# A decoder step with expert retrieval: expert slots in groups of two instead of four, causal key blocks, picks in parts, stages placed by weight

## The chip, the cores and the metric

One core of a Trainium2 chip runs the whole program. The metric is the device time of one execution in microseconds. The page and the traces come from one execution that the hardware profiler recorded.

## The reference

One layer of a decoder for a prompt of 1024 tokens and for 8 sequences of one new token each. All data are float32. For the prompt (the sample goes the same way, with 2048 cached keys for each sequence):

```
xn = rmsnorm(xp)                               # 1024 wide
h  = xn @ w_in                                 # 2240 columns: query latent, key/value latent, rotary key, three conv parts
q_lat, q_rope, ckv, kr = ...                   # 4 heads, latent of 256, rotary part of 64
s = q_lat . ckv + q_rope . kr, masked: key <= query;  p = softmax(s);  o = p @ ckv
xp = xp + concat(norm(o @ w_uv), norm(short_conv(...))) @ w_o
x  = rmsnorm(xp)
q  = x @ w_query                               # 8 heads x 2 halves x 128
s  = q . sub_keys                              # 8 x 2 x 128 scores
sv, si = top_k(s, 16)                          # of each half
top_s, pos = top_k(sv0[:, None] + sv1[None], 16)
experts = si0 * 128 + si1 at pos;  g = softmax(top_s)
u = expert_u[experts];  v = expert_v[experts]  # 8 x 16 = 128 rows of 1024 for each token, twice
a = gelu(x . u)
xp = xp + sum over 128 of (g * a) * v
```

The 128 chosen rows of `expert_u` and the 128 of `expert_v` are 4 KB each, and every token has its own. Outputs are both token groups after a last norm, the new key latents, the new rotary keys and the conv states.

## The kernel before

The prompt is cut into 8 tiles of 128 tokens; a ninth tile holds the 8 sample tokens. Each tile has a **front** (norm, projections, conv, attention, output mix, second norm, eight queries with their top 16, the look-up of the expert numbers) and a **peer** part (128 slots; a slot is one chosen expert of each of the 128 tokens). The front of tile `it+1` is woven into the peer part of tile `it`; the front of tile 0 stands alone at the start, and the sample's small peer part stands alone at the end.

A slot needs two gathers of 512 KB, issued by Pool as indirect DMAs (L1448): rows of `expert_u` into `u_ring`, rows of `expert_v` into `v_ring`, each a ring of `RING` = 8 slots. VectorE multiplies a `u` slot with the tokens and sums (`dot_group`, L1310, which frees the slot in `u_ring`), ScalarE applies gelu, VectorE multiplies with the gates (`weigh_group`, L1316), ScalarE makes a diagonal matrix of it (L933), and TensorE multiplies it with the `v` slot into the accumulator `acc` (`v_group`, L684, which frees the slot in `v_ring`). All of this goes in groups of `G` = 4 slots, 32 groups a tile, with dots one group ahead.

Pool (L1451 to L1471) issues four `u` gathers of the next group, then four `v` gathers of this group, each after a wait for its ring place (`u_free`, `v_free`). It waits for `picked_moved` before slot 0 and for `picks_moved` before slot 64 of a tile.

The order on each engine is written out by hand and is the same on all of them: in group `g`, dots of `g+1` and weights of `g` on VectorE, then the stages of the front that belong to this group; on TensorE the stages, then `v_group(g)`; on ScalarE gelu of `g+1`, diagonals of `g`, then its share of the stages. `beside` (L85) spreads the 31 stages of a prompt front over the first 30 of the 32 groups, one to a group whatever they cost, and the 62 of the sample's front over 31 groups. So `mix_out` is one stage with four weight pieces (L560), a query one stage, a head of the attention one stage, and the last selection (L1245) comes in group 29. The engines wait for each other inside a stage, and each works in order, so whatever follows in its queue waits too.

The attention of the prompt takes all 1024 keys in every tile, with a mask (L1102); keys not yet written are zero from three memsets (L1443). SP loads the weights as 21 pieces a tile, 20 of 1024 KB and one of 768 KB, through a ring of three (`load_w`, L317).

Between tiles VectorE copies the gates and the new tokens to their place (`move_on`, L1318), does two groups of dots, the last norm (`finalize`, L1342) and moves the second half of the picks (`move_picks`, L1331). Seven prompt tiles run in a loop of the engine's own (`Fori`), the eighth is written out.

Before the first gather the opening does all of front 0: projections, four heads, the mix, eight queries and both selections.

## Time and profile before

| | |
|---|---|
| median of three runs | 3765.8 us (3758.39 to 3769.8) |
| the profiled execution | 3753.85 us |
| its span, first to last instruction | 3751.9 us |
| TensorE matmul busy | 2708.7 us (72%), 13848 instructions |
| TensorE weight loads busy | 1557.8 us (42%) |
| VectorE busy | 2310.8 us (62%), 5393 instructions |
| ScalarE busy | 838.7 us (22%) |
| Pool busy | 2332.5 us (62%), 2071 instructions |
| moved | 1321.00 MB, a mean of 352 GB/s over the span |
| mean granted TensorE clock | 0.848 |

Busy time is the time of an engine's instructions; the rest of the span it waits for others or between instructions. DMA share is the part of the time in which the 16 DMA engines had packets under way; it can read slightly over 1 where packets overlap. A row of the timeline gives start, length, engine, line and operation, and in brackets how long the engine had been idle before it and for whom it waited.

### The profile page before, as it was taken

Reading aid. Unit: us, or ns where it says so; the run is one execution under the profiler, and the core shown is the slowest. Engines: PE = TensorE matmul, PEld = TensorE weight load, DVE = VectorE, ACT = ScalarE, POOL = GpSimd, SP = SyncE. Lnnn points to the kernel's source line nnn. Section 1 sums busy time; section 2 is a strip of 40 time slices with the busy share of each in tenths; the row PEclk is TensorE's granted clock in tenths of the full one; section 3 lists DMA queues with packets and bytes.
Section 4 is the critical chain, followed back from the end, with each engine's and each line's share of the span. In section 5 each row is a group of like instructions: output and inputs, shape, how many; then the busy total and the mean of one; then the engine's idle time right before and its main releaser. Section 6 shows DMA issues by size and latency. Waiting matters only on the chain.

```text
span 3751.9 us, 47864 instructions
## 1 busy us (share of the span) xinstructions
PE 2708.7 (72%) x13848; PEld 1557.8 (42%) x13848; DVE 2310.8 (62%) x5393; ACT 838.7 (22%) x2103; POOL 2332.5 (62%) x2071
## 2 busy tenths in 40 slices
PE   7738875687658865797568765887578776988874
PEld 5525442344324532444235432544244433644351
DVE  2374668555875578566865677566856686344474
ACT  1111311222122311232132212131123212123211
POOL 0027776766767676767767776676676776555542
PEclk9878987898878987899779987898889987799876
DMA  5149999999999999999999999999999999999884
GB/s 182 67 161 412 368 401 391 367 400 358 411 359 411 355 404 362 396 372 401 409 348 410 363 411 349 408 361 382 384 376 393 379 409 370 330 331 313 311 308 163
DMA packets 371757, 1321.00 MB, mean 352 GB/s; under 512 B 59684, under 2 KB 78670, under 8 KB 348424
## 3 DMA queue, kind: packets, MB, share of 16 engines
q0 software_dynamic: 297216, 1082.26, 75.2%
q1 hardware_dynamic: 70724, 229.76, 15.9%
q10 hardware_dynamic: 3524, 5.57, 0.4%
q8 instruction: 124, 2.03, 0.2%
q14 instruction: 169, 1.38, 0.1%
HBM read 1311.82 MB, written 5.62 MB: 351 GB/s over the span
## 4 chain that ended last, share of the span: by engine, by line
PE 32%; DVE 32%; DMA 14%; issue 12%; ACT 6%; POOL 2%; SPq 1%; DVEq 1%; ACTq 0%; POOLq 0%
DVE u_ring L1310 12%; PE acc L684 11%; DMA v_ring<-in_expert_v,pick_cur 7%; PE front L410 5%; DMA u_ring<-in_expert_u,pick_cur 4%; PE front L517 3%; PE front L566 3%; PE front L538 2%; ACT diag L933 2%; DVE sv L1201 2%; PE front L518 2%; DVE si_u L1202 2%; DVE work L1201 1%; DMA w_ring<-in_w_pieces 1%; DVE work L1202 1%
## 5 line engine op out<-in xcount | busy, mean ns | idle before, releaser
L1448 POOL DMA_INDIRECT v_ring<-in_expert_v,pick_cur x1024 | 1206.2, 1178 | 687.3 <-PE acc L684 422.4
L684 PE MATMUL acc<-v_ring,diag 128*64 128x512 f32 x4096 | 1188.3, 728 | 592.4 <-ACT diag L933 419.3
L1448 POOL DMA_INDIRECT u_ring<-in_expert_u,pick_cur x1024 | 1106.7, 1081 | 666.2 <-issue 290.5
L1310 DVE CUSTOM_DVE_ANT_0 u_ring<-u_ring,xn_cur 128x1024 f32<-128x1024 f32 x1024 | 1210.6, 1223 | 268.8 <-DMA u_ring<-in_expert_u,pick_cur 253.7
L684 PEld LDWEIGHTS acc<-v_ring,diag 128*64 128x64 f32 x4096 | 348.9, 164 | 1269.2 <-issue 686.6
L410 PE MATMUL front<-work,w_ring 128*128 128x128 f32 (+1 forms) x4896 | 607.2, 283 | 7.0 <-DVE work L1194 5.6
L410 PEld LDWEIGHTS front<-work,w_ring 128*128 128x128 f32 x4896 | 593.0, 201 | 41.6 <-issue 32.6
L926 ACT ACTIVATE gelu<-dots 128x4 f32<-128x4 f32 x256 | 52.7, 206 | 1834.2 <-DVE dots L1310 1833.4
L933 ACT ACTIVATE diag<-ident,wgt 128x64 f32<-128x64 f32 x1024 | 271.5, 336 | 120.7 <-DVE wgt L1316 120.7
L566 PE MATMUL front<-w_ring,work 128*128 128x256 f32 (+1 forms) x576 | 149.7, 426 | 75.5 <-DVE work L1169 65.9
L566 PEld LDWEIGHTS front<-w_ring,work 128*128 128x128 f32 (+1 forms) x576 | 116.2, 205 | 113.3 <-issue 64.2
L1201 DVE MAX8 sv<-work 128x8 f32<-128x128 f32 (+1 forms) x288 | 83.0, 288 | 120.5 <-ACT work L915 103.5
L538 PE MATMUL front<-work,ckv_rows 128*128 128x128 f32 x1024 | 132.6, 292 | 23.2 <-ACT work L879 23.2
L538 PEld LDWEIGHTS front<-work,ckv_rows 128*128 128x128 f32 x1024 | 126.8, 205 | 43.0 <-issue 42.0
L517 PE MATMUL front<-ckvT,rows_next 128*128 128x512 f32 x256 | 125.0, 611 | 1.2 <-ACT rows_next L874 1.2
L417 PE MATMUL front<-ident,work 128*128 128x128 f32 (+1 forms) x72 | 16.8, 408 | 143.7 <-DVE work L1023 143.7
L1102 DVE SCALAR_TENSOR_TENSOR work<-low_keys,small,front 128x512 f32<-128x512 f32 x64 | 45.0, 744 | 101.8 <-PE front L518 101.8
L926 ACT ACT_TABLE_LOAD x83 | 106.5, 1283 | 1.5
L1130 DVE COPY rows_next<-front 128x512 f32<-128x512 f32 x32 | 22.1, 691 | 131.2 <-PE front L624 131.2
L1178 DVE TENSOR_TENSOR rows_next<-front,x_t 128x512 f32<-128x512 f32 (+1 forms) x18 | 11.6, 685 | 125.7 <-PE front L566 125.7
L1202 DVE FIND_INDEX8 si_u<-sv,work 128x8 uint32<-128x128 f32 (+1 forms) x288 | 81.7, 284 | 2.4 <-issue 2.4
L1310 DVE DVE_READ_ACCUMULATOR2_ANT dots<- 128x1 f32 x1024 | 82.3, 80 | 0.0
(242 smaller groups left out, 2382.9 us busy)
## 6 DMA issues: line engine op xcount, KB each, us to landing
w_ring<-in_w_pieces SPq DMA_DIRECT2D x180, 1024.0 KB, 8.4
u_ring<-in_expert_u,pick_cur POOLq DMA_INDIRECT x1024, 12.3
v_ring<-in_expert_v,pick_cur POOLq DMA_INDIRECT x1024, 10.7
work<-in_cache_ckv SPq DMA_DIRECT2D x64, 128.0 KB, 6.2
w_ring<-in_w_pieces SPq DMA_DIRECT2D x9, 768.0 KB, 7.5
x_t<-in_x_prompt SPq DMA_DIRECT2D x8, 512.0 KB
out_y_prompt<-work ACTq DMA_DIRECT2D x8, 512.0 KB
ckv_rows<-in_cache_ckv SPq DMA_DIRECT2D x32, 128.0 KB
```

The lines of the kernel that those rows point to most:

```text
L410: last = nc.tensor.matmul(dst, w[:, k, c0:c0 + m], xT[:, k * T:(k + 1) * T], start=(k == 0), stop=(k == DC - 1))
L517: nc.tensor.matmul(F[half][:, :], q_lat[:, c, h, :], ckvT[:, c, ks], start=(c == 0), stop=False)
L518: last = nc.tensor.matmul(F[half][:, :], q_ro[:, h, :], krT[:, ks], start=False, stop=True)
L538: last = nc.tensor.matmul(F[4][:, c * P:(c + 1) * P], ckv_rows[:, j, c * P:(c + 1) * P], W[1][:, j * P:(j + 1) * P], start=(j == 0), stop= ...
L566: last = nc.tensor.matmul(dst, W[2][:, k * T:(k + 1) * T], w[:, k, :], start=(k == 0), stop=(k == DC - 1))
L684: last = nc.tensor.matmul(acc[rows, half, :], diag[:, s % RING, :], v_ring[:, s % RING, half * 512:half * 512 + 512], start=False, stop=(s ...
L926: nc.scalar.activation(gelu[:, g * G:(g + 1) * G], dots[:, g * G:(g + 1) * G], ACT.Gelu).then_inc(on.gelu_done, 1)
L933: nc.scalar.activation(diag[:, s % RING, :], ident2[:], ACT.Copy, scale=wgt[:, s:s + 1]).then_inc(on.diag_made, 1)
L1201: own(v.max(best, scores), held=True)
L1202: last = v.max_index(index[:, 8 * r:8 * r + 8], best, scores)
L1310: v.tensor_tensor_reduce(u_ring[:, slot, :], u_ring[:, slot, :], xn2_cur[:, block_of(r), :], 1.0, 0.0, ALU.mult, ALU.add, dots[:, g * G + ...
L1448: pool.indirect_dma_start(ring[:, slot, :], None, a[table][0], bass.IndirectOffsetOnAxis(ap=pick, axis=0)).then_inc(loaded[slot], 16)
```

## The change

It touches the order of the work and the attention's extent.

- **Groups of two.** `G` is 2, so 64 groups a tile. Dots run two groups ahead (`AHEAD` = 2, again four slots). Pool still issues bursts of four (`BURST`), `u` of the next four, then `v` of these. `RING` stays 8.
- **Causal key blocks.** Front `f` computes scores, maximum, exp, scaling, turns and values for its `f+1` key blocks of 128 alone; the three memsets go.
- **Finer stages.** The latent projection is three stages of one weight piece, each conv projection two, `mix_out` four. The conv input comes before the turn of the new keys.
- **Picks in parts.** Selection is done in parts of heads: 0 to 3 and 4 to 7 for tiles 1 to 8, and 0 to 1, 2 to 3, 4 to 7 for tile 0. A part's look-up, gates and picks are finished and copied at once, except the last part of tiles after the first, which is copied between the tiles as before. The opening only does the first part of tile 0; its other six queries and two selections are woven into tile 0's slots ahead of front 1.
- **Placing by weight.** `place` spreads the stages by costs in a table (`COST`), over the first 60 of the 64 groups of a prompt tile and the first 62 of the last.
- **Written out.** The loops of tiles are unrolled on all engines, with constants in the waits.
- The order of slots follows: a part's 32 or 64 slots come from its heads alone (`spread_blocks` pairs neighbouring picks).

```diff
-G = 4
+G = 2
 GROUPS = SLOTS // G
-RING = 2 * G
+RING = 8
+AHEAD = 2
+BURST = 4
+def parts_of(f):
+    return [(0, 2), (2, 4), (4, 8)] if f == 0 else [(0, 4), (4, 8)]
+def parts_done(f, part):
+    return sum(len(parts_of(e)) for e in range(f)) + part
+_FIRST = (["norm", "turn"] + [("latent", k) for k in range(3)] + ["latent_norm"] + [("z_in", k) for k in range(2)] + ["kv_rows"]
+          + [("z_gate", k) for k in range(2)] + [("conv", k) for k in range(2)] + ["q_proj", "q_latent"])
+_MIX = ["attn", "mix_norm"] + [("mix_out", k) for k in range(N_OUT)] + ["ffn_norm", "ffn_turn", ("query", 0)]
+COST = {"norm": 0.5, "turn": 0.3, "latent": 0.5, "latent_norm": 0.8, "z_in": 0.7, "kv_rows": 0.2, "z_gate": 0.7, "conv": 0.8, "q_proj": 0.6,
+        "q_latent": 0.4, "head": 1.1, "attn": 0.3, "mix_norm": 1.1, "mix_out": 0.5, "ffn_norm": 0.7, "ffn_turn": 0.3, "query": 0.95, "select": 1.5,
+        "pages": 0.8}
+def _part(f, part):
+    h0, h1 = parts_of(f)[part]
+    return [("query", h + 1) for h in range(h0, h1)] + [("select", part)]
+def front_of(f):
+    return _named(_FIRST + [("head", h) for h in range(H + 1)] + _MIX + _part(f, 0))
+def rest_of(f):
+    return sum([_part(f, part) for part in range(1, len(parts_of(f)))], [])
+def place(stages, span):
+    total, done, groups = sum(COST[s[2]] for s in stages), 0.0, [[] for g in range(GROUPS)]
+    for s in stages:
+        groups[min(int(done * span / total), span - 1)].append(s)
+        done += COST[s[2]]
+    return groups
+def plan(it):
+    if it < TILES - 1:
+        stages = [(0, P) + s for s in rest_of(0)] if it == 0 else []
+        return place(stages + [(it + 1, P) + s for s in front_of(it + 1) + rest_of(it + 1)], GROUPS - 4)
+    f = it + 1
+    stages = _named(_FIRST + [("pages", n) for n in range(SB * QUARTERS + QUARTERS)] + _MIX) + _part(f, 0) + rest_of(f)
+    return place([(f, SB) + s for s in stages], GROUPS - 2)
+def key_blocks(f, half):
+    return min(4, max(0, f + 1 - 4 * half))
...
                 for half in range(2):
-                    ks = slice(half * 512, half * 512 + 512)
+                    ks = slice(half * 512, half * 512 + key_blocks(f, half) * P)
+                    if ks.stop == ks.start:
+                        continue
+                    dst = F[half][:, 0:ks.stop - ks.start]
...
+                if h:
+                    pe.wait_ge(on.olat_kept, n)
                 for c in range(2):
-                    for j in range(TILES):
+                    for j in range(f + 1):
...
-                for g in range(GROUPS):
-                    stages = beside(g, T)
-                    before = 1 if has_pages(stages) else len(stages)
-                    for name, n in stages[:before]:
-                        stage(it + 1, T, name, n)
+                for g, stages in enumerate(PLAN[it]):
+                    for s in stages:
+                        stage(*s)
                     if T != P and g == GROUPS - 1:
                         turn_picks()
                     v_group(it, g)
-                    for name, n in stages[before:]:
-                        stage(it + 1, T, name, n)
...
-            with pe.Fori(0, TILES - 1) as it:
+            for it in range(TILES - 1):
...
-            def select(own, f, T):
+            def move_gates(f, part):
+                h0, h1 = parts_of(f)[part]
+                after(dve, on.w_made, (f - 1) * GROUPS + h1 * TOPK // G if f else 0)
+                return spread_blocks(gate_cur, gate_next, h0 * TOPK // 2, h1 * TOPK // 2)
+            def move_picks(f, part):
+                h0, h1 = parts_of(f)[part]
+                after(dve, on.v_free, RING + (f - 1) * SLOTS + h1 * TOPK if f else 0)
+                spread_blocks(pick_cur, pick_next, h0 * TOPK // 2, h1 * TOPK // 2).then_inc(on.picks_moved, 1)
+            def select(own, f, T, part):
+                hs = slice(*parts_of(f)[part])
...
-                look_up(own, T, 1)
+                look_up(own, T, hs)
...
+                if T == P and (f == 0 or part < len(parts_of(f)) - 1):
+                    assert f == 0 or weighed[0] >= (f - 1) * GROUPS + hs.stop * TOPK // G
+                    own(move_gates(f, part))
+                    move_picks(f, part)
...
             def tile(it, T):
-                own = Own(dve, on.dve_front, (it + 1) * DVE_FRONT)
-                for g in range(GROUPS):
-                    stages = beside(g, T)
-                    half = G // 2 if has_pages(stages) else G
-                    if g and g + 1 < GROUPS:
-                        dot_group(it, g + 1, 0, half)
+                for g, stages in enumerate(PLAN[it]):
+                    if g and g + AHEAD < GROUPS:
+                        dot_group(it, g + AHEAD)
                     if g:
                         weigh_group(it, g)
...
                 if T == P:
-                    move_on(own2, it + 1)
+                    move_on(own, it + 1)
                     dot_group(it + 1, 0)
                     total_square(it, P)
-                    dot_group(it + 1, 1)
+                    for g in range(1, AHEAD + 1):
+                        dot_group(it + 1, g)
                     weigh_group(it + 1, 0)
...
-            pool.memset(ckv_rows[:], 0.0).then_inc(on.zeroed, 1)
-            pool.memset(ckvT[:], 0.0).then_inc(on.zeroed, 1)
-            pool.memset(krT[:], 0.0).then_inc(on.zeroed, 1)
...
-                pool.wait_ge(on.picked_moved, it + 1)
-                gather_group(it, 0, "expert_u", u_ring, u_loaded)
-                for g in range(GROUPS):
-                    if g + 1 < GROUPS:
-                        gather_group(it, g + 1, "expert_u", u_ring, u_loaded)
-                    gather_group(it, g, "expert_v", v_ring, v_loaded)
+                gather_burst(it, 0, "expert_u", u_ring, u_loaded)
+                for first in range(0, SLOTS, BURST):
+                    if first + BURST < SLOTS:
+                        gather_burst(it, first + BURST, "expert_u", u_ring, u_loaded)
+                    gather_burst(it, first, "expert_v", v_ring, v_loaded)
```

## Rows read from the trace of the kernel before

**Rows 1.** The page, moved bytes per second in 40 equal slices of the span.
```profile
GB/s 182 67 161 412 368 401 391 367 400 358 411 359 411 355 404 362 396 372 401 409 348 410 363 411 349 408 361 382 384 376 393 379 409 370 330 331 313 311 308 163
```

**Rows 2.** The page, DMA queues: packets, MB, share of 16 engines.
```profile
q0 software_dynamic: 297216, 1082.26, 75.2%
```

**Rows 3.** Chain of work: start us, us, what; the first projection of each front.
```profile
286.13 10.91 PE front L410 x95
...
3159.86 14.75 PE front L410 x96
```

**Rows 4.** Stretches of the span: length, busy (instructions) by engine, clock, DMA share, GB/s.
```profile
286.13:3159.86 2873.73, 2072.86 (x10368) 1157.36 (x10368) 1895.48 (x4324) 665.67 (x1714) 2017.84 (x1793) 0.86 0.99 385
3159.86:3240.00 80.14, 79.07 (x428) 65.32 (x429) 20.56 (x56) 11.64 (x36) 35.11 (x33) 0.64 0.88 330
3240.00:3514.00 274.00, 239.74 (x1389) 121.90 (x1389) 126.18 (x271) 75.73 (x173) 156.79 (x133) 0.92 0.94 323
3514.00:3690.00 176.00, 127.82 (x610) 74.21 (x609) 119.43 (x350) 31.54 (x87) 80.23 (x69) 0.74 0.72 267
```

**Rows 5.** The same view, 12 us stretches of one tile.
```profile
690.00:702.00 12.00, 10.45 (x54) 6.40 (x55) 7.17 (x15) 2.64 (x7) 6.55 (x8) 0.72 0.95 362
...
834.00:846.00 12.00, 12.00 (x58) 6.05 (x55) 8.21 (x14) 3.95 (x8) 8.49 (x7) 1.00 0.89 314
846.00:858.00 12.00, 8.80 (x49) 5.94 (x48) 10.62 (x21) 4.46 (x10) 8.24 (x6) 0.82 0.83 281
...
942.00:954.00 12.00, 9.92 (x51) 5.13 (x46) 9.76 (x30) 1.15 (x6) 9.58 (x8) 0.72 1.02 413
...
1062.00:1074.00 12.00, 4.22 (x12) 0.94 (x8) 11.52 (x20) 1.27 (x1) 5.89 (x5) 0.64 0.65 221
1074.00:1086.00 12.00, 8.59 (x32) 2.82 (x32) 9.32 (x20) 3.54 (x11) 9.56 (x9) 0.79 0.85 279
```

**Rows 6.** Timeline of Pool, the first gather.
```profile
256.54 1.50 POOL L1448 DMA_INDIRECT u_ring<-in_expert_u,pick_cur  x1 [251.37 <-DVE pick_cur L1226]
```

**Rows 7.** Timeline of VectorE, two heads of the opening.
```profile
106.53 1.40 DVE L1102 SCALAR_TENSOR_TENSOR work<-low_keys,small,front 128x512 f32<-128x512 f32 x2 [5.48 <-PE front L518]
...
109.23 0.15 DVE L1107 TENSOR_SCALAR small<-small 128x1 f32<-128x1 f32 x1
...
118.57 1.41 DVE L1102 SCALAR_TENSOR_TENSOR work<-low_keys,small,front 128x512 f32<-128x512 f32 x2 [5.48 <-PE front L518]
```

**Rows 8.** Timeline of TensorE, opening: the turn of the new keys.
```profile
38.34 0.69 PE L453 MATMUL front<-ident,ck_t 128*128 128x128 f32 x2 [5.28 <-DVE ck_t L1054]
```

**Rows 9.** Timeline of VectorE, opening: queries two and three begin.
```profile
187.50 0.30 DVE L1201 MAX8 sv<-work 128x8 f32<-128x128 f32 x1
...
194.40 0.30 DVE L1201 MAX8 sv<-work 128x8 f32<-128x128 f32 x1
```

**Rows 10.** Timeline of VectorE, opening: one step of a look-up.
```profile
246.03 1.23 DVE L1240 TENSOR_TENSOR work<-work,iota 128x1024 f32<-128x1024 f32 x1
```

**Rows 11.** The page, groups of instructions: busy us, mean ns, idle before.
```profile
L684 PE MATMUL acc<-v_ring,diag 128*64 128x512 f32 x4096 | 1188.3, 728 | 592.4 <-ACT diag L933 419.3
...
L566 PE MATMUL front<-w_ring,work 128*128 128x256 f32 (+1 forms) x576 | 149.7, 426 | 75.5 <-DVE work L1169 65.9
```

**Rows 12.** Groups of instructions, Pool engine, one tile (698.67 to 1108.99).
```profile
L1448 POOL DMA_INDIRECT v_ring<-in_expert_v,pick_cur x129 | 149.4, 1158 | 83.5 <-PE acc L684 49.9 <-issue 33.6
L1448 POOL DMA_INDIRECT u_ring<-in_expert_u,pick_cur x128 | 139.0, 1086 | 44.1 <-issue 36.6 <-DVE dots L1310 6.3 <-PE acc L684 1.2
```

**Rows 13.** Timeline of Pool beside a group of dots: start us, us.
```profile
960.23 0.94 POOL L1448 DMA_INDIRECT u_ring<-in_expert_u,pick_cur  x1 [0.30 <-issue]
961.47 1.77 POOL L1448 DMA_INDIRECT u_ring<-in_expert_u,pick_cur  x1 [0.30 <-issue]
963.55 1.98 POOL L1448 DMA_INDIRECT u_ring<-in_expert_u,pick_cur  x1 [0.30 <-issue]
```

**Rows 14.** Timeline of VectorE, the first of those four dots.
```profile
961.20 1.22 DVE L1310 CUSTOM_DVE_ANT_0 u_ring<-u_ring,xn_cur 128x1024 f32<-128x1024 f32 x1
```

More of the change, by code:

```diff
@@ L72 @@
 QP = NPAGES // QUARTERS
-_FIRST = ["norm", "turn", "latent", "latent_norm", "kv_rows", "z_in", "z_gate", "conv", "q_proj", "q_latent"]
-_LAST = (["attn", "mix_norm", "mix_out", "ffn_norm", "ffn_turn"] + [("query", h) for h in range(PH // 2 + 1)] + [("select", 0)]
-         + [("query", h) for h in range(PH // 2 + 1, PH + 1)] + [("select", 1)])
-STAGES_PROMPT = _FIRST + [("head", h) for h in range(H + 1)] + _LAST
-STAGES_SAMPLE = _FIRST + [("pages", n) for n in range(SB * QUARTERS + QUARTERS)] + _LAST
@@ L80, in stages_of @@
-def stages_of(T):
-    return [s if isinstance(s, tuple) else (s, 0) for s in (STAGES_PROMPT if T == P else STAGES_SAMPLE)]
-def beside(g, T):
-    stages = stages_of(T)
-    span = GROUPS - 2 if T == P else GROUPS - 1
-    return [s for i, s in enumerate(stages) if i * span // len(stages) == g]
+def parts_of(f):
[4 more added lines that the diff above has]
+          + [("z_gate", k) for k in range(2)] + [("conv", k) for k in range(2)] + ["q_proj", "q_latent"])
@@ new lines, with _named @@
+_MIX = ["attn", "mix_norm"] + [("mix_out", k) for k in range(N_OUT)] + ["ffn_norm", "ffn_turn", ("query", 0)]
+COST = {"norm": 0.5, "turn": 0.3, "latent": 0.5, "latent_norm": 0.8, "z_in": 0.7, "kv_rows": 0.2, "z_gate": 0.7, "conv": 0.8, "q_proj": 0.6,
+        "q_latent": 0.4, "head": 1.1, "attn": 0.3, "mix_norm": 1.1, "mix_out": 0.5, "ffn_norm": 0.7, "ffn_turn": 0.3, "query": 0.95, "select": 1.5,
+        "pages": 0.8}
+def _named(stages):
+    return [s if isinstance(s, tuple) else (s, 0) for s in stages]
@@ L95 @@
+def plan(it):
[5 more added lines that the diff above has]
+    return place([(f, SB) + s for s in stages], GROUPS - 2)
+PLAN = [plan(it) for it in range(TILES)]
 LAST = TILES - 1
-def has_pages(stages):
-    return any(name == "pages" for name, n in stages)
@@ L323, in load_tile @@
             def load_tile(f, T):
-                row = sp.snap(f * P)
+                row = f * P
                 load_x(f, T, row)
@@ L349, in _ @@
                 load_w(0, k)
-            with sp.Fori(1, TILES) as f:
+            for f in range(1, TILES):
                 load_tile(f, P)
@@ L788, in _ @@
             nc.tensor.transpose(acc[:, 0, 0:VEC_ROWS], stage_vec, ident[0:VEC_ROWS, 0:VEC_ROWS]).then_inc(on.vec_turned, 1)
-            for name, n in stages_of(P):
+            for name, n in front_of(0):
                 stage(0, P, name, n)
-                if name == "latent":
+                if name == "latent" and n == 2:
                     turn_weights()
@@ L1221, in spread_blocks, with look_up @@
             def spread_blocks(dst, src, first, end):
-                pairs = dst[:, :].rearrange("p (q j) -> p q j", j=2)
+                to = dst[:, :].rearrange("p (q j) -> p q j", j=2)
+                by = src[:, :].rearrange("p (q i) -> p q i", i=2)
                 for i in range(2):
                     for j in range(2):
-                        last = v.tensor_copy(pairs[i * HB:(i + 1) * HB, first:end, j],
-                                             src[j * HB:(j + 1) * HB, i * HB + first:i * HB + end])
-                return last
-            def look_up(own, T, half):
-                hs = slice(half * PH // 2, (half + 1) * PH // 2)
-                grid = [T, PH // 2, TOPK, TOPK]
+                        last = v.tensor_copy(to[i * HB:(i + 1) * HB, first:end, j], by[j * HB:(j + 1) * HB, first:end, i])
+                return last
+            def look_up(own, T, hs):
+                grid = [T, hs.stop - hs.start, TOPK, TOPK]
+                hit = W[0][:, 0:(hs.stop - hs.start) * TOPK * TOPK].rearrange("p (h k a) -> p h k a", k=TOPK, a=TOPK)
                 own(v.tensor_copy(si[0:T, hs], si_u[0:T, hs]))
@@ L1269, in stage @@
                     keep_turned(f, T)
-                elif name == "latent":
+                elif name == "latent" and n == 2:
                     square_latents(f, T)
@@ L1273, in stage @@
                     latents(own, f, T)
-                elif name == "z_gate":
+                elif name == "z_gate" and n == 1:
                     conv_in(own, f, T)
-                elif name == "conv":
+                elif name == "conv" and n == 1:
                     conv(own, f, T)
```

282 lines of the change are left out of this document (128 added, 154 removed).

## The prediction

> **What bounds it now.** I read the page's moved bytes first, then the queues, then stretches, and only then single engines. The reader is to see that from the fourth slice on the core moves 350 to 412 GB/s without a pause [rows 1], and that the gathers are 1082 of the 1321 MB [rows 2]. The chain of work gives the period: the same projection starts at 286.13 and seven tiles later at 3159.86, so a tile takes 410.5 us [rows 3]. Over those seven tiles the DMA share is 0.99 at 385 GB/s, while TensorE is busy 72% and VectorE 66% [rows 4]. A busy DMA can still be badly fed: in a good stretch of 12 us it moves 413 GB/s, in the bad ones 221 to 362 [rows 5]. Most of the 35 such stretches of that tile read 402 to 415, and I take 411 as the full rate. A tile moves 256 gathers of 512 KB, 21.8 MB of weights and 1.2 MB of inputs and outputs, 157.2 MB, which is 382.5 us at 411. So a tile loses 28 us to starved DMA engines. They sit in three places: the heads and the output mix (834 to 882: 2.8 and 3.8 us in the two shown, 12 in all four), the end of the tile with the last query, the selection and the move to the next tile (1062 to 1098 and 690 to 714: 5.5, 3.9 and 1.4 in those shown, 14.6 in all), and 2.4 between [rows 5]; each is 12 x (1 - rate/411).
>
> Around the tiles lie an opening without gathers until 256.54 [rows 6], and after 3159.86 another 592 us, of which 530 at 330, 323 and 267 GB/s [rows 4].
>
> **Opening.** Three edits move the first gather, and all three lie on the path, as Pool has nothing else to wait for [rows 6].
> - Heads. One head takes 12.04 us (106.53 to 118.57), most of it 1024 wide work and 5.48 us of waiting for scores [rows 7]. Front 0 now has one key block instead of eight. The hand-offs stay: five VectorE steps, an exp, a turn and the scores; the smallest step costs 0.15 us [rows 7]. The trace has no head this small, so from below eight such steps with a few hand-offs, 2 us, and from above a third of today's, 5 us. I take 3.3, nearer to the small step because all but the hand-offs shrink by eight: 4 x 8.7 = 35 us less (28 to 40).
> - The conv input comes before the turn of the keys, for which TensorE now idles 5.28 us [rows 8]: 5 less (0 to 6, if its weights are late).
> - Queries and selection. A query takes 6.9 us of VectorE (187.50 to 194.40) [rows 9]. The third begins at 194.40; in its place comes the selection of two heads: six look-up steps of half of 1.23 us [rows 10], 3.7, and some twenty small steps and copies of 0.15 to 0.3, about 4. So the gather comes at about 203 instead of 256.54: 53 less (50 to 56).
>
> Sum: 93 us less (78 to 102); the first gather at about 164. The three memsets on Pool lie under this opening and are worth nothing.
>
> **Tile 0 gets the rest.** Six queries (41 us) and two selections (8 and, with four heads, 12) now lie beside its slots: 61 us of VectorE in the first 13 or so of 64 groups, and six weight pieces, 6.3 MB or 15 us of DMA. Twenty-eight slots and this work ask for about 28 x 1.3 + 61 + weights, 100 us of VectorE; DMA needs 28 x 2.55 + 15 = 86. Cost 20 us: 15 from the bytes, the rest VectorE beyond the rings' slack (15 to 45).
>
> **Seven prompt tiles.** No bytes go, so 382.5 us is the floor. What can be had is the 28.
> - Heads: TensorE has no idle time there (12.00 of 12.00) [rows 5]; a head takes 12.04 us without slots [rows 7] and four slots of matmuls bring it to about 14, against 10.2 of gathers. With `f+1` blocks its 11 or so of TensorE shrink to (f+1)/8. At 2.2 groups a head that is 6 to 13 us for f = 1 to 5 and 14 to 15 for f = 6, 7, against 11.2 of gathers. The first five fronts are covered; the last two keep about 6 us of their loss.
> - Mix: four weight pieces in one group of four slots become four stages over four groups. TensorE's 16.6 us for them (149.7 over nine tiles) and 9.3 for the slots (1188.3 over 1024) [rows 11] then stand beside eight slots, 20 us of gathers and 10 of weights. Covered.
> - End of tile: the last selection goes from group 29 of 32 to 57 of 64, with twelve slots free of stages behind it instead of eight, and half of the picks are long there. But the selection is still one piece of 12 us in which VectorE does no dots, and the move between tiles still stands. I leave half of the 14.6.
> - Hand-offs: twice as many weights, gelus and waits, 32 x 0.2 us more on VectorE and ScalarE, hidden by their 30% and more of idle time [rows 4]; with that cover gone, 6 us a tile.
> - Pool is the cover that is thin. In the tile it is busy 288.4 us for 257 gathers, has 70.2 of issue between them and waits 57 [rows 12]; a gather takes 0.94 us alone and 1.77 and 1.98 beside dots [rows 13, 14]. So Pool alone needs 359 of 382.5 us. Splitting dots into pairs moves where they meet the gathers: from nothing to 0.5 us more for each of 64 pairs (0 to 32 us, so 359 to 391). I take the middle, 375: still under the floor, but Pool can't catch up after a stall.
>
> Together I leave 10 us a tile, and 16 for f = 6 and 7: 5 x 392.5 + 2 x 398.5 = 2759.5 against 2873.7 [rows 4], 114 less; with tile 0's 20, 94 less (10 to 170).
>
> The Trainium skill, page "SBUF — State Buffer", section "Who interferes with whom", has an operation of VectorE with two inputs in SBUF contend only with Pool instructions that read SBUF. The dots are such an operation, and the gathers beside them double, so the row is what I go by; by the rule the gathers would stay at 0.94 where they write only, and Pool would need 318.
>
> **The last tile and the end.** Its first 80 us are TensorE's (79.07 of 80.14, clock 0.64), the next 274 nearly so (239.74) [rows 4]. Splitting shares the projections' time out among slots but doesn't shorten it: 5 less each. In the 176 us that follow DMA share is 0.72; queries two to a group become one to about 2.2 slots: 15 less. The last 62 us stay. Sum 25 less (0 to 50).
>
> **Sum.** 93 + 94 + 25 = 212 less than the profiled execution's 3753.85 (span 3751.9, 2 us around it): 3542. The median of the three runs lies 12 above that execution, so 3554; I say 3550.
>
> **Rivals.**
> - Near the floor: rings and finer stages hide nearly all. Tiles at 384 (186 less), 15 for tile 0, 50 at the end: 3754 - 98 - 186 + 15 - 50 + 12 = 3447. For it: the good stretches; against: selection and the move between tiles remain whole. 0.13.
> - The chains only move: stages wait across engines as before, and lost time comes back where heads and queries now follow closely. Tiles at 405 (38 less), 40 for tile 0, opening 85, end 5: 3754 - 85 - 38 + 40 - 5 + 12 = 3678. For it: four waits of VectorE inside each head remain [rows 7], and Pool can't catch up. The change then does not do in the tiles what it says. 0.2.
> - Memory is the limit: reads of one core cannot go beyond what a tile's mean already shows, 385, so tiles keep 410.5 and only the opening counts: 3754 - 93 + 15 + 12 = 3688. Against: 413 over 12 us and 412 over a whole slice of 94 [rows 1, 5]. 0.02. The Trainium skill gives this rule in "SBUF — State Buffer", section "A bandwidth-pool intuition that's wrong (but worth ruling out)": about 358 GB/s from HBM for a core, and so 3690 us for 1321 MB; the trace disagrees, with 385 over 2874 us.
> - Slower, by Pool: if a pair of dots stretches as many gathers as a burst of four did, two by about 0.95 us each [rows 13], 64 pairs cost 122 us and Pool needs 318 + 122 = 440 a tile. Seven tiles then take 206 more: 3754 - 93 + 206 - 25 + 12 = 3854. It decides from about 427 us of Pool a tile, where the opening and the end are used up. Against: a stretched gather ends with the dots, and two dots last 2.4 us. 0.05.
>
> **Chances.** Forecast 0.6 (3480 to 3620), the others as given. Range 3440 to 3690: it takes in the first three rivals and leaves out the slow one and the tails. Within 0.3%, about what a measurement of this kernel can tell from no change, is 0.02; slower 0.05; faster 0.93.
>
> **What would show it.** First gather at 150 to 180. The same projection's period 388 to 400 for fronts 2 to 5 and more for 6 and 7; tile 0 some 20 longer. Stretches of 12 us under 350 GB/s gone from the heads, still there at the tile's end. Gathers' mean at 1.1 to 1.25 us; above 1.4, Pool has become the bound. TensorE's busy time less by the key blocks. It would be wrong if the period stays over 403, or if Pool has no waits left and the stretches read under 400.

## The result: 3869.7 us, 2.8% slower

The changed kernel takes 3869.7 us (median of four, 3861.4 to 3875.3), the kernel before 3763.0 beside it: ratio 1.028, 95% interval 1.026 to 1.031. The forecast was 3550 with a range of 3440 to 3690: the time lies outside the range, and the sign is wrong too.

The page of the changed kernel (busy time of the engines, and what the DMA moved in the 40 slices), the answer to [rows 1]:

```profile
PE 2687.4 (69%) x13192; PEld 1483.0 (38%) x13192; DVE 2297.9 (59%) x5733; ACT 899.1 (23%) x2374; POOL 2221.2 (57%) x2068
GB/s 177 206 353 377 359 340 307 411 367 381 332 411 359 394 362 355 379 333 382 339 410 314 380 366 348 365 309 385 333 407 294 372 370 338 284 320 294 308 328 202
```

Some work did go: TensorE has 21 us less. Pool has 111 us less with as many gathers; these took less time each, and the memsets are gone. But the slices of tiles 1 to 6 now swing between 294 and 411. In the chain of work stand the first projection of front 2 and, six tiles later, that of the sample's front (compare [rows 3]):

```profile
654.88 4.04 PE front L447 x32
...
3257.73 7.00 PE front L447 x32
```

That is six tiles of 433.8 us, where a tile had 410.5; "over 403" was the prediction's own sign of being wrong. The first gather came as forecast (timeline of Pool, answer to [rows 6]):

```profile
159.48 1.43 POOL L1469 DMA_INDIRECT u_ring<-in_expert_u,pick_cur  x1 [159.02 <-DVE pick_cur L1260]
```

Stretches of 12 us of one tile (busy time of each engine, clock, DMA share, GB/s), the answer to [rows 5]; good stretches still read 408 to 417:

```profile
2053.00:2065.00 12.00, 11.75 (x54) 5.94 (x50) 4.45 (x8) 4.25 (x7) 3.98 (x5) 0.92 0.76 285
2065.00:2077.00 12.00, 9.48 (x32) 4.62 (x33) 5.30 (x12) 3.02 (x8) 8.40 (x8) 0.86 0.66 223
2125.00:2137.00 12.00, 3.52 (x10) 1.28 (x12) 11.86 (x18) 1.49 (x7) 4.94 (x5) 0.57 0.61 225
2245.00:2257.00 12.00, 2.40 (x8) 0.59 (x6) 11.54 (x25) 0.94 (x4) 5.75 (x6) 0.64 0.75 288
2329.00:2341.00 12.00, 7.77 (x26) 2.72 (x28) 11.70 (x31) 3.66 (x16) 2.74 (x3) 0.62 0.34 119
```

These are two heads, the mix norm, the first selection and the last one. In the heads VectorE works 4.5 and 5.3 of 12 us, Pool 4.0 and 8.4, and in the second stretch TensorE isn't full either (9.5): the engines wait for each other. In the last stretch Pool works 2.7 us, on three gathers.

To compare kernels I cut each profiled run at the first gather and at the end of each tile's sum (ScalarE's copy of `acc`), all on chips where the kernel before takes about 3760 us:

| us | before | changed | changed, groups of four | changed, two edits |
|---|---|---|---|---|
| up to the first gather | 256.5 | 159.5 | 158.3 | 160.2 |
| tile 0 | 415.0 | 474.9 | 444.5 | 442.4 |
| tiles 1 to 6 | 2468.0 | 2606.8 | 2438.9 | 2398.0 |
| last tile and end | 612.4 | 627.4 | 637.8 | 606.0 |
| span | 3751.9 | 3868.5 | 3679.5 | 3606.5 |

And inside a tile, what each place lost by moving less than 411 GB/s, as the mean of tiles 1 to 6: the length of each place times (1 - rate/411), cut at the first scores, the attention's last step, the first and last output piece, and the last selection:

| us lost a tile | before | changed | groups of four | two edits |
|---|---|---|---|---|
| projections | 4.6 | 1.7 | 1.9 | 1.5 |
| heads | 7.9 | 18.2 | 7.0 | 4.0 |
| attention's last step, mix norm | 3.6 | 5.9 | 1.1 | 1.0 |
| output mix | 0.5 | 1.6 | 0.7 | 3.7 |
| queries, first selection | 2.1 | 11.0 | 0.5 | 0.5 |
| last selection to the end | 8.2 | 11.9 | 11.3 | 4.4 |
| sum | 26.9 | 50.4 | 22.4 | 15.2 |

The last two columns are experiments 13 and 17 below. Against groups of four the changed kernel loses 28 us more a tile: 11 in the heads, 10.5 between the last output piece and the last selection, 5 at attention's last step and the mix norm. The 11.0 us of the fifth row don't lie between the queries: the queries up to the first selection lose 0.3 together, though most of them too have a group without a stage between them. The first selection and the 12 us behind it lose 6.1, and the rest up to the last selection 4.5.

### The profile page after: what moved, and what is told of

Same layout as the page of the kernel before. It is cut to its first block, busy times and chain, and to the rows that moved or that the text cites. A ratio compares the mean times of both kernels' runs of the same rounds, so it can differ in the third digit from the quotient of the medians.

```text
span 3868.5 us, 43060 instructions
## 1 busy us (share of the span) xinstructions
PE 2687.4 (69%) x13192; PEld 1483.0 (38%) x13192; DVE 2297.9 (59%) x5733; ACT 899.1 (23%) x2374; POOL 2221.2 (57%) x2068
## 4 chain that ended last, share of the span: by engine, by line
PE 38%; DVE 32%; DMA 12%; issue 8%; ACT 6%; POOL 2%; SPq 2%; DVEq 0%; POOLq 0%; ACTq 0%
PE acc L726 17%; DVE u_ring L1354 10%; DMA v_ring<-in_expert_v,pick_cur 9%; PE front L447 6%; DVE si_u L1235 3%; PE front L608 2%; DVE sv L1234 2%; PE front L557 2%; DVE work L1235 2%; ACT diag L972 2%; DVE work L1234 2%; POOL u_ring L1469 1%; PE front L634 1%; DVE work L1273 1%; POOL v_ring L1469 1%
## 5 line engine op out<-in xcount | busy, mean ns | idle before, releaser
L726 PE MATMUL acc<-v_ring,diag 128*64 128x512 f32 x4096 | 1299.3, 770 | 954.4 <-ACT diag L972 753.3
L1469 POOL DMA_INDIRECT v_ring<-in_expert_v,pick_cur x1024 | 1128.8, 1102 | 769.2 <-PE acc L726 502.5
L1469 POOL DMA_INDIRECT u_ring<-in_expert_u,pick_cur x1024 | 1074.1, 1049 | 830.0 <-DVE dots L1354 381.6
L965 ACT ACTIVATE gelu<-dots 128x2 f32<-128x2 f32 x512 | 103.5, 203 | 1656.3 <-DVE dots L1354 1655.3
L1134 DVE SCALAR_TENSOR_TENSOR work<-low_keys,small,front 128x512 f32<-128x512 f32 (+3 forms) x48 | 28.0, 612 | 103.6 <-PE front L558 103.6
L957 ACT COPY work<-front 128x256 f32<-128x256 f32 (+1 forms) x72 | 25.1, 349 | 245.8 <-PE front L447 245.8
L634 PEld LDWEIGHTS front<-sub_keysT,work 128*128 128x128 f32 (+1 forms) x288 | 45.0, 221 | 97.0 <-issue 94.8
L1362 DVE TENSOR_TENSOR wgt<-gelu,gate_cur 128x2 f32<-128x2 f32 x512 | 78.8, 155 | 0.7
L557 PE MATMUL front<-ckvT,rows_next 128*128 128x512 f32 (+3 forms) x192 | 77.6, 530 | 2.3 <-ACT rows_next L910 2.3
L580 PE MATMUL front<-work,ckv_rows 128*128 128x128 f32 x576 | 74.8, 285 | 5.2 <-DVE work L1148 5.2
```

Source lines behind the costliest of these rows:

```text
L557: nc.tensor.matmul(dst, q_lat[:, c, h, :], ckvT[:, c, ks], start=(c == 0), stop=False)
L634: last = nc.tensor.matmul(F[1][0:T, c * KEYS:(c + 1) * KEYS], W[3][:, c * T:(c + 1) * T], sub_keysT[:, c, :], start=True, stop=True)
L726: last = nc.tensor.matmul(acc[rows, half, :], diag[:, s % RING, :], v_ring[:, s % RING, half * 512:half * 512 + 512], start=False, stop=(s ...
L965: nc.scalar.activation(gelu[:, g * G:(g + 1) * G], dots[:, g * G:(g + 1) * G], ACT.Gelu).then_inc(on.gelu_done, 1)
L1362: v.tensor_tensor(wgt[:, s], gelu[:, s], gate_cur[:, s], ALU.mult).then_inc(on.w_made, 1)
L1469: pool.indirect_dma_start(ring[:, slot, :], None, a[table][0], bass.IndirectOffsetOnAxis(ap=pick, axis=0)).then_inc(loaded[slot], 16)
```

## What happens between two heads

TensorE's timeline over one period of the heads (start, length):

```profile
2059.93 2.94 PE L580 MATMUL front<-work,ckv_rows 128*128 128x128 f32 x24
2062.81 1.94 PE L726 MATMUL acc<-v_ring,diag 128*64 128x512 f32 x8
2067.52 2.74 PE L726 MATMUL acc<-v_ring,diag 128*64 128x512 f32 x8 [2.78 <-ACT diag L972]
2070.20 1.54 PE L567 MATMUL front<-ident,work 128*128 128x128 f32 x6
2071.53 2.09 PE L557 MATMUL front<-ckvT,rows_next 128*128 128x512 f32 x4
...
2075.66 0.70 PE L558 MATMUL front<-krT,q_ro 64*128 64x256 f32 x2
```

and VectorE's over the same time:

```profile
2063.65 0.62 DVE L1142 TENSOR_SCALAR work<-work,small 128x768 f32<-128x768 f32 x1
2064.19 1.22 DVE L1354 CUSTOM_DVE_ANT_0 u_ring<-u_ring,xn_cur 128x1024 f32<-128x1024 f32 x1
...
2066.48 0.16 DVE L1362 TENSOR_TENSOR wgt<-gelu,gate_cur 128x2 f32<-128x2 f32 x1
...
2071.35 0.69 DVE L1148 COPY work<-front 128x512 f32<-128x512 f32 x1 [2.35 <-PE front L567]
2076.39 1.14 DVE L1134 SCALAR_TENSOR_TENSOR work<-low_keys,small,front 128x512 f32<-128x512 f32 x2 [4.35 <-PE front L558]
```

The probabilities are ready at 2064.27. The next head's turns (L567) start at 2070.20. Between them stands the group without a stage: heads lie two groups apart, so in TensorE's queue the matmuls of the group in between (2067.52) come ahead of the turns. They wait for a diagonal, this for weights (2066.48), and these stand on VectorE behind two dots. Only then come turns and scores, and VectorE waits 2.35 and 4.35 us for them. In the kernel before each of the first 30 groups had a stage, and nothing that waits for fresh work stood between a head and the next.

The Trainium skill, page "PSUM — Partial Sum Buffer", section "Engine vs sequencer instructions", has matmuls start and complete in program order. The trace agrees: turns whose input was ready at 2064.27 stayed behind matmuls released at 2067.52.

From one head's maximum to the next there are as a rule four slots in all kernels. For front 7, where all key blocks count and the work is that of before, the three distances are 12.0, 14.1, 14.1 us before and 19.2, 17.1, 17.1 in the changed kernel. From ready probabilities to turns it is 1.6 us before, in every tile, and 5.0 to 7.1 in the changed kernel (means of a tile).

The changed kernel holds a test of this by itself. In front 1 the third and fourth head stand in neighbouring groups, with no group between them. There the turns start 0.5 us after the probabilities, and the heads are 4.9 us apart; the other three waits of that front are 6.2 to 6.9 us.

## Experiments

The kernel before takes 3760 to 3764 us on some chips and 3930 to 3968 on others, so between sets only ratios to it on the same chip are compared, and absolute times only within one set. Two theories stand behind the expectations. "Reach": when a long stage of VectorE begins, TensorE can only multiply the slots already weighed, two instead of four. "Queue between heads": the reading of the last section. The expectations of the first set had a chip in mind on which the changed kernel takes 3870; on the chip that they met it would take about 3970 to 3990, by its ratios in the next sets (1.001 and 1.005). So the absolute bands of these four don't apply, and the ratios are read.

**First set: three ways out of the groups of two (before: 3968.3).** Groups of four (stages over 30 of 32 groups, 31 in the last tile):

```diff
-G = 2
+G = 4
-AHEAD = 2
+AHEAD = 1
```

> The changed kernel with groups of four again (dots one group ahead, stages over 30 of 32 groups, 31 in the last tile); short opening, key blocks, finer stages, picks in parts and the placing by cost stay. Two theories put the loss on the groups of two. Reach: when a long stage of VectorE begins, only the two slots already weighed can still be multiplied on TensorE and set free, where it was four. Queue between heads: the group without a stage between two heads puts two dots, a weighing, a diagonal and its matmuls ahead of the next head's turns, about 5.5 us for each head (cycle of 16 us for four slots in the changed kernel's trace, 10.2 needed). By either the tile period falls from 421 to 444 back to about 400 to 412, and the time to about 3640 to 3720 us. Third theory, that it isn't the group size but the other edits (key blocks, parts, placing, loops written out): the periods stay near 421 to 444 and the time at 3820 to 3880.

Measured 3864.6, ratio 0.975 (0.970 to 0.979). Weights and diagonals one group earlier (with a second group of both at the start of a tile):

```diff
-                    if g:
-                        weigh_group(it, g)
+                    if g and g + 1 < GROUPS:
+                        weigh_group(it, g + 1)
...
-                    if g:
-                        diag_group(it, g)
+                    if g and g + 1 < GROUPS:
+                        diag_group(it, g + 1)
```

> The changed kernel, in which VectorE weighs and ScalarE makes the diagonals of group g+1 in group g, one group earlier than now, so that four slots are ready for TensorE when a stage begins; nothing else moves. Reach: the dips under 350 GB/s in the heads, the mix norm and the selections become shallower, loss of a tile from 38 to 61 us down to about 25, time 3650 to 3730. Queue between heads: the heads lose their coupling too (the group between them needs no fresh dots), the rest stays; 20 us a tile less, about 3720 to 3750. Other edits are the cause: within 20 us of 3870.

Measured 3765.8, ratio 0.951 (0.947 to 0.955). TensorE's matmuls one group later:

```diff
-                    v_group(it, g)
+                    if g:
+                        v_group(it, g - 1)
+                v_group(it, GROUPS - 1)
```

> The changed kernel, in which TensorE does the matmuls of group g-1 instead of g after the stages of group g. This takes the waiting matmuls out of the way of the next head's turns, but frees each v slot later by a group. Queue between heads: the heads' cycle falls from 16 to 11 or 12 us, 20 us a tile less, time about 3720 to 3750. Reach: the v slots come free later in every long stage, mix norm and selections lose more, the heads gain a little; time 3830 to 3950. Other edits: within 20 of 3870.

Measured 3749.7, ratio 0.945 (0.941 to 0.949). Weights ahead of the dots in the same group (the two calls swapped, and the diagonals ahead of the gelu):

> The changed kernel, in which VectorE weighs group g before the dots of g+2 instead of behind them, and ScalarE makes the diagonals before the gelu. It takes 2.4 us of dots out of the path from a stage's end to the matmuls, but gives TensorE no more slots during a stage. Queue between heads: 2.4 of 5.5 us for each head, and as much after each long stage: 10 to 15 us a tile less, about 3770 to 3800. Reach: the same 2.4 us after each stage at most, as dips are set by the two slots, 3800 to 3860. Other edits: within 20 of 3870.

Measured 3808.2, ratio 0.960 (0.957 to 0.964).

The third edit separates the theories: it moves the freeing of every v place behind another group's stages, so by reach it should have gained nothing, and it was the best of the four. The queue between heads stands, and the traces show it at the place itself. In front 7 the heads are 18.9, 17.1 and 17.1 us apart in the changed kernel on a chip of this kind (experiment 5); with weights ahead they are 12.2, 14.1 and 14.1 apart, the distances of the kernel before, and with the matmuls late 14.8, 12.1 and 14.1.

The gains are larger than I gave them. Between the last output piece and the last selection a tile loses 2.3 us with weights ahead and 1.9 with the matmuls late, where the changed kernel loses 13 to 14 on such chips. So that loss comes from the order too, but which wait carries it there wasn't traced.

**Second set: controls, both edits, all keys (before: 3929.7).**

> The changed kernel as it is, as a control beside the others and beside the kernel before on the same chip, which took 3968 us on the chip of the last four runs and 3763 on that of the result. If a chip only scales the time, the ratio is 1.028 again, on a chip like the first about 3870, on one like the second about 4080. If the groups of two are to blame for all that the last four variants gained, it is 4 to 8 per cent over them.

Measured 3948.7, ratio 1.005 (1.002 to 1.008): on such a chip the change costs little, as the kernel before loses more there too: 46 us a tile in its trace below instead of 27, while the changed kernel goes from 50 to 62.

> The kernel before as it is, for its trace on this chip. Ratio 1.00. If it takes about 3763 us, its tiles have 410 us again and full stretches at 411 GB/s; if it takes about 3968, the trace shows what is slower there: lower rates throughout (the gathers' memory), or dips in places (a transfer or a code fetch that comes late).

Measured 3932.5. Its good stretches read 409 to 414 GB/s as elsewhere; its tiles take 424 to 438 us and lose 39 to 54, with dips in the same places. ScalarE's copy of a query (L919) waits 332 us in all, where it waited 60. Why these chips let dips grow is open.

> The changed kernel with both edits: weights and diagonals of g+1 in group g, and TensorE's matmuls of g-1 after the stages of g. If reach decides, this has as much reach as weights ahead alone, but v places come free two slots later: 0 to 40 us slower than that one (3766 on the last chip). If the waiting matmuls in front of the next stage decide, both edits take away the same wait, and together they give no more than the better one (3750). If the two losses are separate, it is 30 to 60 us faster than either.

Measured 3690.6, ratio 0.937 (0.932 to 0.943), 6.5% under the control. Separately they had 0.951 and 0.945: together they give 1 to 1.5% more than one alone did on the other chip, so most of what they remove seems to be the same wait; the two sets ran on different chips.

Attention over all keys (with the three memsets):

> The changed kernel with attention over all 1024 keys in every tile, as before. Opening 30 us longer. If the spacing of heads decides (a group without a stage between them), each head's cycle is about 17 to 18 us for four slots in all tiles, as in the last one; tiles of 444 to 450 us throughout instead of 421 to 444, and the time about 100 to 130 us above the changed kernel. If key blocks were to blame (their growth from tile to tile is a mark of it), the tiles fall back towards 410 us and the time towards 3790.

Measured 4085.0, ratio 1.035 (1.026 to 1.043). By the ratios that is about 116 us above the control. The profiled execution, 4109.9, was the longest of the four and lies 147 above the control's, so its parts are somewhat too large: 38 in the opening, 21 in tile 0, 84 in tiles 1 to 6. The key blocks are a gain. The heads are 17.1 to 19.8 us apart here in every front from 1 on, but for the two in neighbouring groups (12.4), as they are in front 7 of the changed kernel: with key blocks the period grows from tile to tile because the work in each head does.

**Third set: size against placing (before: 3968.3).**

> The changed kernel once more, as the control for the three variants beside it: they have to be read on one chip, since the ratio to the kernel before was 1.028 on one chip and 1.005 on another. Time 3860 to 3960, ratio 1.00 to 1.03.

Measured 3964.8, ratio 1.001.

> Groups of four again beside the control. It was 0.975 of the kernel before on one chip, about what the short opening is worth alone. If the size of the groups is the main loss, it is 2.5 to 5 per cent under the control (which was 1.005 and 1.028 of before elsewhere), and its tiles are as long as those of the kernel before, though not shorter, since attention's last step and the mix norm now follow each other in one group. If the placing is the main loss, it is within 1 per cent of the control.

Measured 3873.9, ratio 0.974 (0.968 to 0.979): 91 us or 2.3% under the control, a little less than the 2.5 to 5 I had written, but well over the 1% of placing. It is also less than either remedy gave on a chip of this kind. In the changed kernel attention's last step and the mix norm share a group. VectorE's timeline there:

```profile
2108.70 1.21 DVE L1354 CUSTOM_DVE_ANT_0 u_ring<-u_ring,xn_cur 128x1024 f32<-128x1024 f32 x1
...
2114.48 1.23 DVE L1191 TENSOR_TENSOR work<-mo 128x1024 f32<-128x1024 f32 x1 [4.49 <-ACT mo L942]
2119.08 1.29 DVE L1039 TENSOR_SCALAR work<-front 128x512 f32<-128x512 f32 x2 [3.37 <-PE front L598]
2123.93 1.22 DVE L1034 TENSOR_TENSOR work<-work 128x1024 f32<-128x1024 f32 x1 [3.56 <-ACT work L859]
...
2130.11 1.22 DVE L1354 CUSTOM_DVE_ANT_0 u_ring<-u_ring,xn_cur 128x1024 f32<-128x1024 f32 x1
```

Twenty us without a dot. Parting them:

```diff
-"attn": 0.3,
+"attn": 1.1,
```

> The changed kernel with one number changed: the cost of the attention's last step from 0.3 to 1.1, so that it and the mix norm stand in groups of their own with slots between. In the changed kernel's trace the two form one stretch of 20 us of VectorE (2109.91 to 2130.19) without a dot. If this pile is what starves the rings there, each tile's dip at the mix (225 GB/s over 12 us, 5.4 us lost, and 333 beside it, 2.3) shrinks by half: 3 to 5 us a tile, 25 to 40 us in all. If the order of weights and matmuls is all that matters, it gives less than 10 us.

Measured 3952.7, ratio 0.997 (0.994 to 1.001): 12 us less than the control, whose own ratio is 1.001 (0.996 to 1.005). That is no more than the measurement can tell, and the pile is not the cause.

> Weights one group ahead, TensorE's matmuls a group later, attention's last step apart, the mix norm in two stages and each selection in two (half of the look-up each). With the first two alone 0.937 of the kernel before. If long stages of VectorE are what is left, the dips at the mix and the selections shrink and it is 0.915 to 0.93 of before (a tile 393 to 400 us on a chip like the last). If what is left is the heads and the end of a tile, it is the same 0.937.

Measured 3688.3, ratio 0.927 (0.922 to 0.932). This lies in the band that I gave to the long stages, but the 0.937 it is held against came from another chip. The fifth set, with both versions on one chip, decides otherwise.

**Fourth set, on a chip like that of the result (before: 3760.1).**

> Groups of four in the changed kernel, as a control on this chip: 0.974 of the kernel before as on two others, or 0.99 to 1.00 if this chip is like the first.

Measured 3682.4, ratio 0.980 (0.977 to 0.984), between the two values that I had named. Against the changed kernel's 1.028 the groups of two cost about 187 us on such chips: in the table above 30 in tile 0 and 168 in tiles 1 to 6, with 10 given back at the end.

> Groups of four with TensorE's matmuls of group g-1 after the stages of g. If the gain of this edit with groups of two (0.945 of before, where the control stood at 1.00 to 1.03) came from the stageless groups between two stages, there is next to nothing to gain here, and each v place comes free four slots later with a ring of eight: the same as the control to 60 us slower. If it helps because it simply parts TensorE's waiting matmuls from VectorE's work in every group, it is 60 us or more faster than the control.

Measured 3891.1, ratio 1.037 (1.033 to 1.041): 209 us over its control, far more than the 60 I had allowed. The same edit that gave 0.945 with groups of two loses 5.7% where nearly every group has a stage. Pool's and VectorE's longest waits, first of groups of four, then with the matmuls late (us in total, times, longest):

```profile
POOL v_ring L1469 <- PE acc L726: 587.2, 214, 27.8
DVE u_ring L1354 <- DMA u_ring<-in_expert_u,pick_cur: 378.9, 128, 10.3
```

```profile
POOL v_ring L1471 <- PE acc L726: 864.8, 197, 25.9
DVE u_ring L1356 <- DMA u_ring<-in_expert_u,pick_cur: 716.7, 203, 16.7
```

A v place that comes free four slots late, in a ring of eight, holds up Pool, and with it the u gathers behind it. So I read these waits; no run with a longer ring was made.

> Weights ahead, matmuls later, attention's last step, mix norm and selections apart: 0.927 of the kernel before again on a chip like the last; 0.94 to 0.96 on a chip like the first, where the kernel before loses less.

Measured 3622.6, ratio 0.965 (0.961 to 0.968), just above the 0.94 to 0.96.

> The same with Pool's gathers in bursts of two u and two v instead of four. In the trace of the version with weights ahead Pool stood 13.6 us before a u gather in the mix norm while v places had come free. If Pool's order holds up the v gathers, 5 to 10 us a tile come back, 30 to 70 us in all. If u and v places come free together after a long stage, it is within 15 us.

Measured 3765.4, ratio 1.001: 143 us slower than the run beside it, against both cases that I had written down. Waits of bursts of four, then of two:

```profile
POOL v_ring L1487 <- PE acc L726: 426.4, 146, 13.8
DVE u_ring L1370 <- DMA u_ring<-in_expert_u,pick_cur: 471.1, 146, 11.3
```

```profile
POOL v_ring L1487 <- PE acc L726: 749.7, 231, 17.1
DVE u_ring L1370 <- DMA u_ring<-in_expert_u,pick_cur: 666.7, 276, 11.4
```

With bursts of two, Pool reaches a v gather whose place isn't free with two u gathers fewer issued ahead of it; VectorE then waits for u twice as often. That the shorter lead of u is the reason is read from these rows, not tested by itself.

**Fifth set, another chip of that kind (before: 3764.3).**

> Weights ahead and matmuls later alone. 0.937 of the kernel before on one chip of the slower kind. On a chip of the faster kind, where all three edits gave 0.965: 0.965 to 0.975.

Measured 3613.6, ratio 0.962 (0.959 to 0.964). TensorE's timeline at a head of the same front:

```profile
1912.09 3.65 PE L726 MATMUL acc<-v_ring,diag 128*64 128x512 f32 x16
1916.56 0.87 PE L567 MATMUL front<-ident,work 128*128 128x128 f32 x6 [0.81 <-DVE work L1145]
```

Four slots of matmuls in one piece, then TensorE stands waiting for the probabilities of the front's first head, not they for it. Behind the second and third head the turns wait 2.1 to 2.6 us in fronts 4 to 7, about what they waited before (2.1), and in front 7 the heads are 12.2, 14.1 and 14.1 us apart, exactly as before. TensorE's wait for diagonals fell to 119 us in all; it now waits 479 us for v data, so here the transfers are what holds it.

> The same with attention's last step apart, the mix norm and the selections in two stages. If the long stretches still starve the rings, 10 to 40 us under the run beside it; if the rings and the two other edits already cover them, within 8 us of it.

Measured 3628.2, ratio 0.965 (0.963 to 0.968): 15 us over the run beside it, outside both bands that I had given. Parting the long stretches brings nothing any more, and may cost a little. So the version to keep is the one with two edits, 3.8% faster than the kernel before and 6.5% than the changed one by their ratios (0.962 and 1.028).

## Why the prediction was wrong, step by step

- **Opening: right.** 97 us less, forecast 93. A head of front 0 takes 4.05 us (forecast 3.3, bounds 2 to 5), a query 6.9.
- **Hand-offs: the step that failed.** The prediction said "32 x 0.2 us more on VectorE and ScalarE, hidden by their 30% and more of idle time", and 6 us a tile without that cover. It counted instructions. What halving the groups changed was the order in the queues: stages are placed once in two groups, and the group between them puts a wait for VectorE in front of TensorE's next stage. That is 3.4 to 5.5 us for each head (5.0 to 7.1 against 1.6). Idle time of VectorE couldn't hide it, since VectorE idled because of it. Groups of two cost 28 us a tile (2606.8 against 2438.9 over six), where I had nothing to 6. The heads are 11 of the 28, and attention's last step with the mix norm 5. Some 10 more fall at and after the first selection; the order is to blame there as well, since each remedy takes most of it away, but through which wait is open.
- **The groups are not all of the miss.** With groups of four the span is 72 us shorter than before, not 212: the opening gives 98 and tiles 1 to 6 give 29 together, where I had 16 for each tile, and tile 0 and the end take 55 back. With the two edits tiles 1 to 6 give 70. So what a tile could gain was put too high even without the groups' cost.
- **Heads.** I had 6 to 13 us a head for f = 1 to 5 and 14 to 15 for 6 and 7. With groups of four the distances are 7.2 to 12.6 (and 7.0 once, with no slot between) and 10.8 to 14.1: the estimate of the key blocks was right. In the changed kernel they are 10.6 to 16.6 (and 4.9 once, with two slots between) and 17.1 to 19.2.
- **Mix: "covered" was right for the output pieces**, 1.6 us lost a tile; beside it I missed that the placing puts attention's last step and the mix norm into one group, 20 us without a dot. Parting them alone gave 12 us, within the noise.
- **End of the tile.** I left half of 14.6; in the table's cut it went from 8.2 to 11.9, and to 11.3 with groups of four. "Twelve slots free of stages behind it" gave nothing: VectorE does the last query from 2308.57 to 2315.32 and the selection from 2320.10 to 2329.84, with four dots between, and then the next eight dots without a wait. So eight slots of `u` had long been loaded, with no place free: Pool stands from 2328.42 to 2337.65 waiting for a v place, and TensorE, which frees it, waits 7.96 us for a diagonal. Nothing is left to transfer (119 GB/s in the stretch from 2329).
- **Tile 0.** Forecast 20 more (15 to 45), measured 60, and 29.5 with groups of four: three quarters of the miss of 40 is the groups again.
- **The last tile and the end.** Forecast 25 less, measured 15 more, and 25 more with groups of four. The new code no longer splits a page stage's dots in halves around it; whether that is the reason was not tried. With two edits it is 6 less.
- **Pool: the rival "slower, by Pool" is refuted.** Its 3854 lies 16 us from the measured time, but that is luck: its reason was wrong. The page of the changed kernel, the answer to [rows 11, 12]:

```profile
L1469 POOL DMA_INDIRECT v_ring<-in_expert_v,pick_cur x1024 | 1128.8, 1102 | 769.2 <-PE acc L726 502.5
L1469 POOL DMA_INDIRECT u_ring<-in_expert_u,pick_cur x1024 | 1074.1, 1049 | 830.0 <-DVE dots L1354 381.6
L726 PE MATMUL acc<-v_ring,diag 128*64 128x512 f32 x4096 | 1299.3, 770 | 954.4 <-ACT diag L972 753.3
```

  Gathers got shorter (1102 and 1049 ns against 1178 and 1081), below the 1.1 to 1.25 us that I had given, and Pool waits more. The argument against this rival, "a stretched gather ends with the dots", was wrong as well: in the changed kernel 90 of the 225 gathers over 1.5 us end 0.7 to 0.9 us behind them. TensorE's wait for diagonals, 419 us before, is now 753.
- **"The chains only move"** named the place, the waits inside each head, but put a tile at 405 us, below the 410.5 of before; it was 433.8. I took the distance of the stages in slots (4.4 to a head instead of 4) and not what stands between them in each queue.

Put together: opening -97, tile 0 +60, tiles 1 to 6 +139, last tile and end +15, which is +117 on the spans (3868.5 against 3751.9).

## What to carry to other kernels

When work is interleaved by hand on engines that work in order, look at what stands between two dependent stages in each queue, not at the sum of what is added. If finer groups leave some without a stage, their matmuls must be ready before they come up: weigh a group earlier or let the consumer run a group late. The second remedy, the late consumer, cost 209 us where nearly every group had a stage and a group filled half of the ring.

## What the runs showed of the hardware

- Chips differ by 4 to 6% on the kernel before (3760 to 3764 us on three, 3930 to 3968 on three others) with about the same 411 GB/s in good stretches; the changed kernel's ratio moves from 1.028 to 1.001 with them.
- A gather beside a pair of dots can still take about twice as long (1.84 us at 2065.52, 0.94 alone). As many gathers meet a dot as before (871 of 2064, before 877), but on average these now take 1.23 us instead of 1.36; the others take 0.96 in both kernels. The Trainium skill, page "SBUF — State Buffer", section "Who interferes with whom", has such an operation contend with Pool instructions that read SBUF, not with those that only write it. A gather reads its row numbers from `pick_cur`, which is a tile in SBUF, so the rows don't go against this rule, as the prediction took them to do; no run here has a Pool instruction beside dots that only writes.
